# Normalising the second block's windowed attention after the fact: one inversion for all sums, spread by matmul during the merge gates

## The chip, the cores and the metric

The program runs on one core of one Trainium2 chip. The metric is the device time of one execution, in microseconds (us). The engines run side by side, each through its own queue in order: TensorE (PE, with weight loads shown apart as PEld), VectorE (DVE), ScalarE (ACT), GpSimd (POOL) and the queue that issues most transfers (SP). They meet only at semaphores.

## The reference

Two blocks run one after the other on a sequence of 512 tokens of width 1024. The change lies in the second one: a windowed attention with 16 query heads on 4 key heads, whose softmax has a learned sink in its denominator, and the gated merge behind it.

```python
def one_block(args):                      # one block of 128 queries; q, k, v of 64 per head
    s_loc = einsum('bqkrd,bskd->bkrqs', qn, kn) * scale, masked to the window
    s_ctx = einsum('bqkrd,bskd->bkrqs', qn, k_ctx) * scale
    logits = concatenate([s_loc, s_ctx])
    m = maximum(max(logits), sink_l)
    p = exp(logits - m)
    denom = sum(p) + exp(sink_l - m)
    return einsum('bkrqs,bskd->bqkrd', p / denom, vals)
...
y_b = window_gqa(qh, kh, vh, k_ctx, v_ctx, attn_sink)
g_a, g_b = split(sigmoid(h @ w_in[gates] + b_merge_gate))
merged = g_a * (y_a @ w_proj_a) + g_b * (y_b @ w_proj_b)
x = x + g1 * (merged @ w_out)
# then: router, top-64 tokens for each of 16 experts, expert products, final norm
```

`p / denom` may be formed behind the product with the values as well, since `denom` belongs to a query and a head alone.

## The kernel before

**The attention loop.** It walks 16 units: 4 key heads by 4 blocks of 128 queries. A unit has four query heads and a window of `nb` = 4 blocks of keys (first and last query block) or 5. Work of three units overlaps. In step i of the loop each engine does, in this order:

- PE: scores of unit i, first pair of heads (`att_scores`, L1167 and L1178); two turns (transposes, L1201) of the probabilities of unit i-1; scores of the second pair; the other turns; then `att_values` of unit i-2 (L1221). At its end, before: four fp32 matmuls (L1228), which spread the reciprocals of the four heads' sums over 64 partitions and 128 queries, into the other half of the bank that holds the values. In the trace each fp32 matmul leaves two records.
- DVE: the inversion of unit i-1's sums (`att_recip`, L2551 and L2552), mask and maximum of unit i (L2534, L2535, L2539), the sink's argument (L2543), some evictions of turned probabilities (L2558), then `att_out` of unit i-2: a copy of the values (L2567) and the multiplication by the spread reciprocals (L2568). Units 4 to 7 in addition have a quarter of `gate_low` each (L2575).
- ACT: three evictions of turned probabilities (L1917), four exponentials with their sums (L1907), the sink's exponential (L1913); in four steps a quarter of `gate_high` (L1927).

The last steps of the loop hold the first three tiles of the first merge gate (`first_gate`), so that PE has work while the last probabilities come.

**The merge behind it.** Eight products in the order of `MERGE`: gate a 0, gate a 1, gate b 0, gate b 1, proj a 0, proj a 1, proj b 0, proj b 1. Each is four tiles of 24 matmuls (L810; 8 steps of k by three products of rounded parts). Each product's 128 x 4096 weights are split first: ACT writes the rounded high part (L1552), DVE the rest, the low part (L2039), and PE waits for `low_ready`. There are two slots for high parts that take turns: the split for product n+1 is begun on ACT when product n-1 is done on PE. ACT evicts the gate tiles with a sigmoid (L1484). DVE has nothing between the splits until the branches are rounded at the fourth gate product.

**PSUM banks.** `plan_banks` gives each tile of the merge, in order, the next of eight banks. `claim` makes PE wait until the tile that had the bank before is evicted (`freed_a`, `freed_d` count ACT's and DVE's evictions in their order).

## Time and profile before

| | us |
|---|---|
| median of 3 runs | 2354.07 |
| the 3 runs | 2354.07, 2354.26, 2347.15 |
| the profiled execution | 2349.28 |
| its span on the core | 2346.8 |
| the attention loop in it | 1038 to 1181 |
| the merge and out projection in it | 1181 to 1399 |
| routing and experts in it | 1399 to the end |

What lies outside the profiled span is 2349.28 - 2346.8 = 2.5 us. PE is busy 95% of the span, DVE 40%, ACT 26%, POOL 6%; the mean granted TensorE clock is 0.98 of full speed. Such a share is an average over stages, so the text below reads the attention loop and the gate products by themselves: first how busy each engine is there, then the chain of work that ended last, then single instructions in order of time.

### The profile page before, as it was taken

To read this page: it belongs to the slowest core of one execution; us is meant where nothing else is said; L and a number is where in the kernel's file an instruction comes from. 1 tells how busy PE (TensorE), PEld (TensorE's weight loads), DVE (VectorE), ACT (ScalarE), POOL (GpSimd) and SP (SyncE) were. 2 spreads that over 40 slices of the span, in tenths; PEclk is the share of its full clock that TensorE was granted. 3 is DMA by queue.
4 is the path that set the end of the run, shared out by engine and by line. 5 is a ranking of instruction groups with operands and counts; after the bars stand their busy time and mean duration, and the time that the engine had idled before them with its cause. 6 is when DMAs were issued, how large, how long until landed. Compare 5 with 4: busy or idle time off the path is not lost.

```text
span 2346.8 us, 25253 instructions
## 1 busy us (share of the span) xinstructions
PE 2223.7 (95%) x10940; PEld 1465.5 (62%) x10940; DVE 947.9 (40%) x1313; ACT 603.4 (26%) x858; POOL 143.8 (6%) x138
## 2 busy tenths in 40 slices
PE   7999999999999999999999998999898989898998
PEld 5887888878888888887788883434242424242433
DVE  4848435478887353798624322111111101110011
ACT  5315233343333254336533221000000000000001
POOL 0231000310000010320000210000000000000000
PEclk9999999999999999999999998999999999999999
DMA  7220434435454342220023249999999999999997
GB/s 307 105 78 32 166 144 179 161 144 205 160 209 170 118 144 101 88 72 1 1 72 108 96 193 365 429 435 430 430 433 430 429 433 430 430 432 431 429 430 296
DMA packets 55948, 571.88 MB, mean 244 GB/s; under 512 B 3808, under 2 KB 3936, under 8 KB 36000
## 3 DMA queue, kind: packets, MB, share of 16 engines
q1 hardware_dynamic: 51392, 524.55, 54.1%
q0 software_dynamic: 3152, 28.71, 3.3%
q10 hardware_dynamic: 1296, 17.04, 1.9%
q8 instruction: 86, 1.41, 0.2%
q14 instruction: 22, 0.18, 0.0%
HBM read 568.18 MB, written 2.10 MB: 243 GB/s over the span
## 4 chain that ended last, share of the span: by engine, by line
PE 36%; DMA 18%; DVE 3%; ACT 1%; issue 1%; DVEq 0%; SPq 0%; ACTq 0%
PE ps L1359 10%; PE ps L810 9%; DMA arena<-in_w_exp_up 8%; PE ps L1455 6%; DMA arena<-in_w_exp_gate 4%; DMA weights<-in_w_exp_gate 3%; PE ps L1332 3%; DVE arena L2156 2%; DMA weights<-in_w_exp_down 1%; PE ps L1201 1%; PE ps L1221 1%; DMA weights<-in_w_exp_up 1%; PE ps L1379 1%; PE ps L1167 1%; PE ps L1400 1%
## 5 line engine op out<-in xcount | busy, mean ns | idle before, releaser
L810 PE MATMUL ps<-weights_r 128*128 128x512 f32 (+1 forms) x2656 | 813.5, 386 | 8.2 <-DVE hT_r L2059 4.3
L810 PEld LDWEIGHTS ps<-weights_r 128*128 128x128 f32 x2656 | 495.5, 188 | 114.9 <-issue 7.9
L810 PE MATMUL ps<-hT_r,weights_r 128*128 128x512 f32 x1264 | 462.0, 390 | 0.0
L1359 PE MATMUL ps<-weights,arena 128*64 128x512 f32 x768 | 352.1, 615 | 50.7 <-DMA weights<-in_w_exp_up 36.6
L1361 PE MATMUL ps<-weights,arena 128*64 128x512 f32 x768 | 352.4, 616 | 0.0
L2039 DVE TENSOR_TENSOR weights_r<-weights,weights_r 128x4096 fp32r<-128x4096 f32 (+1 forms) x45 | 192.7, 4282 | 223.0 <-ACT weights_r L1552 221.2
L1359 PEld LDWEIGHTS ps<-weights,arena 128*64 128x64 f32 x768 | 105.6, 141 | 283.1 <-issue 246.5
L810 PEld LDWEIGHTS ps<-hT_r,weights_r 128*128 128x128 f32 x1264 | 237.7, 188 | 48.8
L810 PE MATMUL ps<-arena_r,weights_r 128*128 128x512 f32 (+1 forms) x768 | 243.8, 387 | 0.0
L1552 ACT ACTIVATE weights_r<-weights 128x4096 fp32r<-128x4096 f32 (+1 forms) x46 | 161.6, 3512 | 217.4 <-PE ps L810 114.5
L2711 DVE TENSOR_TENSOR hT<-hT,ps 128x512 f32<-128x512 f32 x32 | 22.0, 688 | 438.9 <-PE ps L1361 438.9
L1455 PE MATMUL ps<-weights,hT 128*64 128x512 f32 x384 | 168.6, 594 | 0.6 <-DMA weights<-in_w_exp_down 0.6
L1458 PE MATMUL ps<-weights,hT 128*64 128x512 f32 x384 | 168.5, 594 | 0.0
L810 PEld LDWEIGHTS ps<-arena_r,weights_r 128*128 128x128 f32 x768 | 144.2, 188 | 29.3
L1359 PE MATMUL ps<-arena 128*64 128x512 f32 x248 | 112.8, 608 | 16.3 <-DMA arena<-in_w_exp_up 13.3
L1455 PEld LDWEIGHTS ps<-weights,hT 128*64 128x64 f32 x384 | 51.1, 137 | 109.1 <-issue 105.9
L1361 PE MATMUL ps<-arena 128*64 128x512 f32 x256 | 116.2, 608 | 0.0
L2696 DVE SCALAR_TENSOR_TENSOR xT<-ps,mod_cols,xT 128x512 f32<-128x512 f32 x56 | 42.0, 751 | 165.8 <-PE ps L1379 160.6
L1361 PEld LDWEIGHTS ps<-weights,arena 128*64 128x64 f32 x768 | 105.7, 141 | 0.0
L2078 DVE SCALAR_TENSOR_TENSOR weights<-weights,arena 128x1024 f32<-128x1024 f32 x80 | 94.3, 1224 | 13.5 <-DMA weights<-in_w_ada 11.0
L1999 ACT ACTIVATE hT<-ps 128x512 f32<-128x512 f32 x32 | 16.5, 599 | 292.6 <-PE ps L1400 292.6
L1359 PEld LDWEIGHTS ps<-arena 128*64 128x64 f32 x248 | 33.8, 140 | 91.5 <-issue 66.3
(326 smaller groups left out, 2379.6 us busy)
## 6 DMA issues: line engine op xcount, KB each, us to landing
weights<-in_w_exp_down SPq DMA_DIRECT2D x21, 4096.0 KB, 31.6
weights<-in_w_exp_gate SPq DMA_DIRECT2D x21, 4096.0 KB, 27.5
weights<-in_w_exp_up SPq DMA_DIRECT2D x21, 4096.0 KB, 28.5
weights<-in_w_in SPq DMA_DIRECT2D x18, 2048.0 KB, 7.9
arena<-in_w_exp_down SPq DMA_DIRECT2D x7, 4096.0 KB, 31.7
arena<-in_w_exp_gate SPq DMA_DIRECT2D x7, 4096.0 KB, 31.1
arena<-in_w_exp_up SPq DMA_DIRECT2D x7, 4096.0 KB, 31.4
weights<-in_w_up SPq DMA_DIRECT2D x11, 2048.0 KB, 8.0
```

Source lines behind the costliest of these rows:

```text
L810: last = pe.matmul(t, a if w_first else b, b if w_first else a, start=(k == 0 and n == 0), stop=(k == kt - 1 and n == len(pairs) - 1))
L1167: local = pe.matmul(ps[:, c:c + w], q2[o:o + 64, 2 * kv + p, n * P:(n + 1) * P], kdup[o:o + 64, kv, b0 * P:b1 * P], start=True, stop=True)
L1332: last = pe.matmul(bank(6, 2)[:, d * P:(d + 1) * P], h2_tok[:, t, 256 * j + r:256 * j + 256:2], sels[it % 2][:, t, :], start=(t == 0), sto ...
L1359: la = pe.matmul(bank(b0 + n)[0:64, :], xe[:, 2 * j + r, 0:64], ra[:, n * 512:(n + 1) * 512], start=start, stop=stop)
L1361: lb = pe.matmul(bank(b0 + n)[64:128, :], xe[:, 2 * j + r, 64:128], rb[:, n * 512:(n + 1) * 512], start=start, stop=stop)
L1455: la = pe.matmul(bank(4 + hh)[0:64, :], hmid_t[:, 4 * j + r, 0:64], w[:, r, 0, hh * 512:(hh + 1) * 512], start=(j + r == 0), stop=(j == ST ...
L1458: lb = pe.matmul(bank(4 + hh)[64:128, :], hmid_t[:, 4 * j + r, 64:128], w[:, r, 1, hh * 512:(hh + 1) * 512], start=(j + r == 0), stop=(j = ...
L1552: A(slots_r[high_slot(i)][:, 0:n], slots[sl][:, 0:n], ACT.Copy).then_inc(S["high_ready"], 1)
L2039: ve.tensor_tensor(slots_r[sl][:, 0:n], slots[sl][:, 0:n], slots_r[high_slot(i)][:, 0:n].bitcast(F32), ALU.subtract).then_inc(S["low_ready ...
L2078: last = ve.scalar_tensor_tensor(w[:, j, :], w[:, j, :], 1.0, rows[:, 0, :], ALU.mult, ALU.mult, accum_out=cc[:, 4 * c + j, 0:1])
L2156: last = ve.tensor_tensor(rsinbuf[q:q + 32, i % 2, :], plain[o:o + 32, :], cs[o:o + 32, 1, :], ALU.mult)
L2696: ve.scalar_tensor_tensor(xT[:, d, :], ps[:, b * 512:(b + 1) * 512], mod_cols2[:, 40 + d, 0:1], xT[:, d, :], ALU.mult, ALU.add).then_inc(S ...
```

## The change

The new code keeps the values of every unit as they come from PSUM (`att_out` is one copy) and keeps all maxima and sums of the 16 units in the arena (`neg_m`, `den`, 4 blocks by 16 heads each). Behind the loop `att_recips` on DVE and `att_sinks` on ACT form all 64 denominators per query at once, invert them, and split the result in a high and a low part. `turn_reciprocals` on PE turns both (32 rows: 16 high, 16 low) into one bank, ACT evicts it as `rden_t`, and behind the second gate product `spread_reciprocals` multiplies it with a matrix of ones and zeros (`head_sel`), one fp32r matmul for each of the eight 128-row tiles of the values. `scale_values` on DVE multiplies these tiles, straight from PSUM, into the values. ACT's rounding of the branch waits for that.

```diff
@@ plan_banks, merge
             for n in range(4):
                 b.add((tag, kind, part, nq, n), "A" if kind == "gate" else "D")
+            if (tag, i) == ("m2", 0):
+                b.add("rdenT", "A")
+                b.skip(7)
+            if (tag, i) == ("m2", 1):
+                for k in range(KT):
+                    b.add(("rden", k), "D")
@@ PE, merge
                         feature_tiles(name, tiles[done:], h_parts, c0=done * P)
+                        if (tag, i) == ("m2", 0):
+                            turn_reciprocals()
+                        if (tag, i) == ("m2", 1):
+                            spread_reciprocals()
@@ PE, att_values
-                pe.wait_ge(S["r_ready"], i + 1)
-                for a in range(2):
-                    for g in range(2):
-                        r = 2 * a + g
-                        last = pe.matmul(t[64 * g:64 * g + 64, 256 + a * P:256 + (a + 1) * P],
-                                         rden[:, i % 2, r:r + 1].broadcast_to([P, 64]), ident,
-                                         start=True, stop=True)
+            def turn_reciprocals():
+                pe.wait_ge(S["r_ready"], 1)
+                t = claim(pe, "rdenT")
+                for n in range(TT):
+                    last = pe.transpose(t[0:2 * NH, n * P:(n + 1) * P], unit_rows[:, n, :], ident)
+                fill("rdenT", last)
+            def spread_reciprocals():
+                wait_freed(pe, "rdenT")
+                for k in range(KT):
+                    sel = head_sel[0:2 * NH, 2 * k:2 * k + 2, :].rearrange("p h d -> p (h d)")
+                    fill(("rden", k), pe.matmul(claim(pe, ("rden", k)), sel, rden_t[0:2 * NH, :],
+                                                start=True, stop=True))
@@ ACT, merge_gates
+                    if (tag, i) == ("m2", 0):
+                        free("rdenT", "A", A(rden_t[0:2 * NH, :], wait_full(act_e, "rdenT")[0:2 * NH, :], ACT.Copy))
...
-                            act_e.wait_ge(S["pv_free"], UNITS)
+                            wait_freed(act_e, ("rden", KT - 1))
@@ ACT, attention
-                    if i >= 2:
-                        act_e.wait_ge(S["r_ready"], i - 1)
...
-            def att_sink(i):
-                act_e.wait_ge(S["sink_arg"], i + 1)
-                act_e.wait_ge(S["exp_done"], 4 * i + 4)
-                A(sink_e[:, i % 2, :], sink_t[:, i % 2, :], ACT.Exp).then_inc(S["sink_exp"], 1)
+            def att_sinks():
+                act_e.wait_ge(S["sink_arg"], 1)
+                A(neg_m, neg_m, ACT.Exp).then_inc(S["sink_exp"], 1)
+                act_e.wait_ge(S["den_summed"], 1)
+                A(rden_high, den, ACT.Copy).then_inc(S["rden_high"], 1)
...
+            att_sinks()
             act_e.wait_ge(S["pv_full"], 2 * UNITS)
             merge_gates("m2", 3)
@@ DVE, merged_tiles
                     prepare((tag, kind, part, nq))
+                    if (tag, i) == ("m2", 2):
+                        scale_values()
@@ DVE, attention
-            def att_recip(i):
-                ve.wait_ge(S["sink_exp"], i + 1)
...
-                link(ve.tensor_tensor(rden[:, i % 2, :], den[:, i % 2, :], sink_e[:, i % 2, :], ALU.add))
-                ve.reciprocal(rden[:, i % 2, :], rden[:, i % 2, :]).then_inc(S["r_ready"], 1)
+            def att_recips():
+                ve.wait_ge(S["nm_ready"], 2 * UNITS)
+                ve.wait_ge(S["exp_done"], 4 * UNITS)
+                ve.tensor_tensor(neg_m, neg_m, wide(sink.unsqueeze(1), P, TT, NH), ALU.add)   # sink_arg
+                ve.tensor_tensor(head_sel[0:2 * NH, :, :], ...)                               # 32 x 1024
+                ve.wait_ge(S["sink_exp"], 1)
+                link(ve.tensor_tensor(den, den, neg_m, ALU.add))
+                ve.reciprocal(den, den).then_inc(S["den_summed"], 1)
+                ve.wait_ge(S["rden_high"], 1)
+                ve.tensor_tensor(rden_low, den, rden_high.bitcast(F32), ALU.subtract).then_inc(S["r_ready"], 1)
+            def scale_values():
+                ve.wait_ge(S["pv_free"], UNITS)
+                for k in range(KT):
+                    t = wait_full(ve, ("rden", k))
+                    free(("rden", k), "D", ve.tensor_tensor(q2[:, k, :], t, q2[:, k, :], ALU.mult))
@@ DVE, att_out
-                link(ve.tensor_copy(v, t[:, 0, :, :]))
-                ve.tensor_tensor(v, v, t[:, 1, :, :], ALU.mult).then_inc(S["pv_free"], 1)
+                ve.tensor_copy(q2[:, 2 * kv:2 * kv + 2, n * P:(n + 1) * P],
+                               ps[:, 7 * 512:7 * 512 + 256].rearrange("p (a q) -> p a q", a=2)).then_inc(
+                    S["pv_free"], 1)
```

PE's queue at the end of the loop and around the first gate products, before (L1221 values of the last unit, L1228 their reciprocals, L810 gate tiles; the rows with waits are the heads of tiles 2 and 3 of gate a 0, tile 0 of gate a 1, and tile 0 of gate b 0):

```order
L1221 MATMUL ps<-weights,arena 64x256 [waits pv_free,at_kept_d,at_kept_a]
L1221 MATMUL ps<-weights,arena 64x256 x7
L1228 MATMUL ps<-cst,small 64x128 [waits r_ready]
L1228 MATMUL ps<-cst,small 64x128 x3
L810 MATMUL ps<-weights_r 128x512 [waits freed_a,low_ready]
...
L810 MATMUL ps<-weights_r 128x512 [waits freed_d,low_ready]
...
L810 MATMUL ps<-weights_r 128x512 [waits freed_a,low_ready]
```

The same queue of the changed kernel (L1234 values, L819 gate tiles, L1245 the turn, L1253 the spreading), first to the head of gate a 1, then to the head of gate b 0:

```order
L1234 MATMUL ps<-weights,arena 64x256 [waits pv_free,at_kept_d,at_kept_a]
L1234 MATMUL ps<-weights,arena 64x256 x7
L819 MATMUL ps<-weights_r 128x512 [waits freed_a,low_ready]
...
L1245 MATMUL ps<-cst,arena 32x128 [waits freed_d,r_ready]
L1245 MATMUL ps<-cst,arena 32x128 x3
L819 MATMUL ps<-weights_r 128x512 [waits freed_a,low_ready]
...
L1253 MATMUL ps<-arena_r 128x512 [waits freed_a] x8
L819 MATMUL ps<-weights_r 128x512 [waits freed_d,low_ready]
```

The four matmuls of each unit are gone, four transposes and eight spreading matmuls stand between the gate products, and gate b 0 now waits for a bank that DVE frees. In the plan that bank is the one of `("rden", 0)`; gate a 1 takes the bank of `rdenT`, which ACT frees.

DVE's queue from the last values on, before (L2567 and L2568 values, L2039 low parts of the weights, L2181 the first branch):

```order
L2567 COPY arena<-ps 128x2x128 [waits pv_full]
L2568 TENSOR_TENSOR arena<-arena,ps 128x2x128 [waits dve_chain]
L2039 TENSOR_TENSOR weights_r<-weights,weights_r 128x4096 [waits high_ready] x4
L2181 TENSOR_TENSOR arena_r<-arena,arena_r 128x512 [waits branch_high] x4
L2181 TENSOR_TENSOR arena_r<-arena,weights_r 128x512 [waits branch_high] x4
```

and of the changed kernel (L2570 to L2578 are `att_recips`, L2063 the low parts, L2585 is `scale_values`):

```order
L2598 COPY arena<-ps 128x2x128 [waits pv_full] x2
L2570 TENSOR_TENSOR arena<-arena,small 128x4x16 [waits exp_done,nm_ready]
L2572 TENSOR_TENSOR arena_r<-cst 32x1024
L2575 TENSOR_TENSOR arena<-arena 128x4x16 [waits sink_exp]
L2576 RECIPROCAL arena<-arena 128x4x16 [waits dve_chain]
L2578 TENSOR_TENSOR arena_r<-arena,arena_r 128x4x16 [waits rden_high]
L2063 TENSOR_TENSOR weights_r<-weights,weights_r 128x4096 [waits high_ready] x3
L2585 TENSOR_TENSOR arena<-ps,arena 128x512 [waits tile_full,pv_free]
L2585 TENSOR_TENSOR arena<-ps,arena 128x512 [waits tile_full] x7
L2063 TENSOR_TENSOR weights_r<-weights,weights_r 128x4096 [waits high_ready]
```

The eight multiplications stand behind three low parts: those for gate a 1, gate b 0 and gate b 1. On ACT the two new instructions (L1935, L1937) stand between the last eviction of probabilities and the high part for gate a 1.

## Rows read from the trace of the kernel before

**Rows 1.** Page: granted TensorE clock, tenths of full speed, 40 slices of 58.7 us.
```profile
PEclk9999999999999999999999998999999999999999
```
**Rows 2.** Windows: us, busy time (x records) of each engine, granted clock, DMA share, GB/s.
```profile
1060.00:1100.00 40.00, 38.03 (x318) 28.37 (x320) 32.89 (x67) 29.32 (x69) 0.00 (x0) 1.00 0.00 1
1195.00:1215.00 20.00, 20.00 (x90) 16.57 (x89) 4.43 (x1) 4.52 (x6) 0.00 (x0) 1.00 0.23 87
```
**Rows 3.** Chain that ended last, one unit: start us, us, what.
```profile
1137.52 0.44 PE ps L1228 x8
...
1142.41 0.61 ACT arena L1917
1143.01 0.14 issue
1143.15 1.95 PE ps L1221 x16
1145.10 0.44 PE ps L1228 x8
```
**Rows 4.** Timeline, seam between two units: start us, us, engine, line, operation.
```profile
1096.64 2.38 PE L1221 MATMUL ps<-weights,arena 128*64 128x256 f32 x20
1098.82 0.64 PE L1228 MATMUL ps<-cst,small 128*64 128x128 f32 x8
1099.39 0.70 PE L1167 MATMUL ps<-arena 64*128 64x256 f32 x4
```
**Rows 5.** Timeline, end of the attention loop and first gate product.
```profile
1181.27 3.63 ACT L1552 ACTIVATE weights_r<-weights 128x4096 fp32r<-128x4096 f32 x1 [11.05 <-PE ps L1228]
1181.27 0.42 DVE L2567 COPY arena<-ps 128x256 f32<-128x256 f32 x1 [7.17 <-PE ps L1228]
1184.94 4.42 DVE L2039 TENSOR_TENSOR weights_r<-weights,weights_r 128x4096 fp32r<-128x4096 f32 x1 [2.78 <-ACT weights_r L1552]
1192.38 0.69 ACT L1484 ACTIVATE arena<-ps,cols 128x512 f32<-128x512 f32 x1 [4.32 <-PE ps L810]
```
**Rows 6.** Timeline, seam between gate a 1 and gate b 0.
```profile
1208.70 0.69 ACT L1484 ACTIVATE arena<-ps,cols 128x512 f32<-128x512 f32 x1 [4.75 <-PE ps L810]
1214.14 0.69 ACT L1484 ACTIVATE arena<-ps,cols 128x512 f32<-128x512 f32 x1 [4.75 <-PE ps L810]
1214.73 3.62 ACT L1552 ACTIVATE weights_r<-weights 128x4096 fp32r<-128x4096 f32 x1
1218.38 4.43 DVE L2039 TENSOR_TENSOR weights_r<-weights,weights_r 128x4096 fp32r<-128x4096 f32 x1 [17.33 <-ACT weights_r L1552]
```
**Rows 7.** Single lines: duration ns min/median/max, first and last start us, forms.
```profile
L2204 DVE TENSOR_TENSOR arena<-ps,arena x32: 684/692/692, 387.9 to 1344.8; 128x512 f32<-128x512 f32 x32
L1960 ACT ACTIVATE hT<-ps x1: 587/587/587, 1404.6 to 1404.6; 16x512 f32<-16x512 f32 x1
L2325 DVE RECIPROCAL arena<-arena x8: 3342/3344/3347, 181.8 to 224.0; 128x512 f32<-128x512 f32 x8
L2575 DVE TENSOR_TENSOR weights_r<-weights,weights_r x4: 1218/1218/1219, 1092.6 to 1115.6; 128x1024 fp32r<-128x1024 f32 x4
```
**Rows 8.** Windows (columns as in rows 2): PE idle, then at work again.
```profile
1036.00:1038.00 2.00, 1.05 (x9) 0.88 (x9) 1.75 (x5) 1.92 (x6) 0.00 (x0) 1.00 0.00 0
1052.00:1053.00 1.00, 1.00 (x6) 1.00 (x6) 0.00 (x0) 1.00 (x4) 0.00 (x0) 0.50 0.00 0
1406.00:1407.00 1.00, 1.00 (x10) 1.00 (x9) 0.93 (x4) 1.00 (x3) 0.00 (x0) 0.87 0.88 377
1686.00:1687.00 1.00, 1.00 (x6) 0.29 (x4) 0.00 (x0) 0.00 (x0) 0.00 (x0) 0.92 0.84 360
```
**Rows 9.** Timeline, first matmuls behind three waits of PE; in brackets idle us and releaser.
```profile
1050.15 0.92 PE L1167 MATMUL ps<-arena 64*128 64x384 f32 x4 [1.80 <-ACT weights L1907]
1402.06 1.02 PE L1284 MATMUL ps<-cst,arena 128*16 128x128 f32 x4 [1.27 <-DVE arena L2624]
1682.42 0.84 PE L1359 MATMUL ps<-weights,arena 128*64 128x512 f32 x1 [2.54 <-DMA weights<-in_w_exp_up]
```

More of the change, by code:

```diff
@@ L333, in build_two_blocks @@
             merged_ready pair_in0 pair_in1 pair_in2 pair_in3 up_halves_in conv_mid gelu_ready act_ready ln_ready ln_stats ln_root ya_ready exp_done
-            kdup_ready as_half as_full nm_ready sink_arg sink_exp at_full at_kept_a at_kept_d
+            kdup_ready as_half as_full nm_ready sink_arg sink_exp at_full at_kept_a at_kept_d den_summed rden_high
             r_ready pv_full pv_free row_ready aff_exp router_in router_w aff_ready rank_ready sel_ready wsel_full
@@ L699, in build_two_blocks @@
         nsink = small[:, 64:80]
-        neg_m, den, sink_e, rden, sink_t = (small[:, 80 + 8 * j:88 + 8 * j].rearrange("p (b r) -> p b r", b=2)
-                                            for j in range(5))
+        unit_rows, unit_rows_r = at(17920, TT, 2 * NH), at(17920, TT, 2 * NH, rounded=True)
+        den, neg_m = unit_rows[:, :, 0:NH], unit_rows[:, :, NH:2 * NH]
+        rden_low, rden_high = unit_rows_r[:, :, 0:NH], unit_rows_r[:, :, NH:2 * NH]
+        head_sel = at(16896, NH, HD, rounded=True)
+        rden_t = at(16384, L, rounded=True)
         tops = small[:, 120:124].rearrange("p (b g) -> p b g", b=2)
@@ L1220, in att_values @@
                     for g in range(2):
-                        pe.matmul(t[64 * g:64 * g + 64, 0:256].rearrange("p (a q) -> p a q", a=2),
-                                  vals[:, kv * HD:(kv + 1) * HD], pt[:, g, b, :, :],
-                                  start=(b == 0), stop=(b == nb - 1))
-                pe.wait_ge(S["r_ready"], i + 1)
-                for a in range(2):
-                    for g in range(2):
-                        r = 2 * a + g
-                        last = pe.matmul(t[64 * g:64 * g + 64, 256 + a * P:256 + (a + 1) * P],
-                                         rden[:, i % 2, r:r + 1].broadcast_to([P, 64]), ident,
-                                         start=True, stop=True)
-                        if a == 1:
-                            last.then_inc(S["pv_full"], 1)
+                        last = pe.matmul(t[64 * g:64 * g + 64, 0:256].rearrange("p (a q) -> p a q", a=2),
+                                         vals[:, kv * HD:(kv + 1) * HD], pt[:, g, b, :, :],
+                                         start=(b == 0), stop=(b == nb - 1))
+                        if b == nb - 1:
+                            last.then_inc(S["pv_full"], 1)
+            def turn_reciprocals():
[10 more added lines that the diff above has]
+                                                start=True, stop=True))
             def first_gate(n):
@@ L2536, in att_max @@
                                       ps[:, c:c + 2 * nb * P].rearrange("p (g s) -> p g s", g=2), AX.X, ALU.max))
-                if i >= 2:
-                    ve.wait_ge(S["sink_exp"], i - 1)
-                ve.scalar_tensor_tensor(neg_m[:, i % 2, 2 * p:2 * p + 2], tops[:, p, :], -1.0, nsink[:, h:h + 2],
+                ve.scalar_tensor_tensor(neg_m[:, n, h:h + 2], tops[:, p, :], -1.0, nsink[:, h:h + 2],
                                         ALU.mult, ALU.min).then_inc(S["nm_ready"], 1)
-                if p:
-                    ve.wait_ge(S["nm_ready"], 2 * i + 2)
-                    ve.tensor_tensor(sink_t[:, i % 2, :], neg_m[:, i % 2, :], sink[:, 4 * kv:4 * kv + 4],
-                                     ALU.add).then_inc(S["sink_arg"], 1)
-            def att_recip(i):
-                ve.wait_ge(S["sink_exp"], i + 1)
-                if i >= 2:
-                    ve.wait_ge(S["pv_full"], 2 * (i - 1))
-                link(ve.tensor_tensor(rden[:, i % 2, :], den[:, i % 2, :], sink_e[:, i % 2, :], ALU.add))
-                ve.reciprocal(rden[:, i % 2, :], rden[:, i % 2, :]).then_inc(S["r_ready"], 1)
+            def att_recips():
+                ve.wait_ge(S["nm_ready"], 2 * UNITS)
+                ve.wait_ge(S["exp_done"], 4 * UNITS)
+                ve.tensor_tensor(neg_m, neg_m, wide(sink.unsqueeze(1), P, TT, NH), ALU.add).then_inc(
+                    S["sink_arg"], 1)
+                ve.tensor_tensor(head_sel[0:2 * NH, :, :], wide(ident[0:2 * NH, 0:NH].unsqueeze(2), 2 * NH, NH, HD),
+                                 wide(ident[0:2 * NH, NH:2 * NH].unsqueeze(2), 2 * NH, NH, HD), ALU.add)
+                ve.wait_ge(S["sink_exp"], 1)
[8 more added lines that the diff above has]
+                    free(("rden", k), "D", ve.tensor_tensor(q2[:, k, :], t, q2[:, k, :], ALU.mult))
             def att_keep(i, u):
@@ L2592, in _ @@
                     late_context_keys()
-                if 0 < i <= UNITS:
-                    att_recip(i - 1)
                 if i < UNITS:
@@ L2606, in _ @@
                     gate_low(i - 6)
+            att_recips()
             merged_tiles("m2")
```

6 lines of the change are left out of this document (2 added, 4 removed).

## The prediction

> **What bounds the kernel now.** I read the stage of the change first, by windows. In the attention loop PE is busy 38.03 of 40 us, DVE 32.89, ACT 29.32, and the granted clock is full; between the gate products behind it PE is busy all the time [rows 2]. So PE sets the pace in both, and what it is spared or made to do counts. The remaining 5% of the loop is in the chain that ended last [rows 3]: in each unit it runs on PE, leaves it for one eviction on ACT (0.61 us and 0.14 of issue), and comes back for the values and the four matmuls of L1228 (eight records). These stand in the chain with 0.44 us in 14 of the 16 units (the rows show two of them). The two others are the first, where DVE's and ACT's work is the chain, and the one at 1161, behind which PE waited for the last exponentials in any case. Outside this stretch I need the page's clock line (full nearly throughout [rows 1]) only to know that a dip there would be new. The experts' stage streams weights, but PE's progress frees its buffers and the routing in front of it is serial, so I let a shift of PE at 1181 or 1214 go through to the end undiminished.
>
> **What goes from the loop.** Four matmuls per unit. The timeline gives more than the chain's 0.44: their first record starts at 1098.82, the next scores at 1099.39, that is 0.57 us of PE's queue [rows 4]. The values' records in front run at (1098.82 - 1096.64) / 20 = 0.109 us each, with no gap before L1228, while 0.14 us of the 0.57 lie between the last of L1228 and the scores. The switch to the scores may need that gap behind the values too; but their weights could also be loaded while the values still run, since their waits are over by then. I take 0.57, with 0.44 and 0.66 (the same seam counted from the weight loads) as ends. 14 units: 14 x 0.57 = **8.0 us gained** (6.2 to 9.2).
>
> The Trainium skill speaks for less: its page "TensorE: Matmul & The Clock Gate", section "Wait — 56ns, not 53.3ns?", has back-to-back matmuls of 128 columns start 55.6 ns apart at full clock. Eight would take 0.44 us, as the chain says and not as the starts say; by it the gain would be 6.2 us.
>
> DVE is spared a 128 x 256 multiplication and three small instructions a unit, ACT one exponential. Neither is the bound, so I count nothing; where ACT stands in the chain (four units with a quarter of a high part) up to 1.5 us more may come, kept for the range. DVE also gets slack, so it does not become late next when PE goes 0.57 us faster per unit of 8: it has 7 us in 40 to spare already [rows 2].
>
> **What comes between the loop and gate a 1.** In the changed order ACT's high part for gate a 1 stands behind two instructions that hang on DVE, and DVE's denominators behind the last copy of values. Before, both started at 1181.27 and the low part was ready at 1184.94 + 4.42 = 1189.4, while PE needed it at about 1192.0 (0.4 us before ACT evicts tile 3, 1192.38 [rows 5]): 2.6 us to spare. Now ACT starts after: the copy 0.42, a small sum 0.2, `head_sel` (32 x 1024; nearest row 1.22 [rows 7]), another small sum 0.2, a reciprocal of 64 columns (3.344 / 512 x 64 = 0.42, with a fixed part some 0.55 [rows 7]), a small copy 0.25, and six handoffs of 0.05: 3.1 us later. That alone would use up the slack and 0.5 us more. But PE itself comes later: four transposes, then gate a 1 takes the bank of `rdenT`, which ACT evicts behind tile 3. So 1192.38 + 0.69 + 0.587 (a 16 x 512 eviction [rows 7]) + 0.05 = 1193.7 against 1192.0, on the old clock of times. The wait for the bank covers the late low part: **1.7 us lost**, about 1.2 of it idle. Lower end 1.2, if the eviction of 32 rows overlaps the sigmoid's end; if `head_sel` took 0.5 more, the cover would still hold.
>
> **What comes between gate a 1 and gate b 0.** Eight spreading matmuls of 512 columns: 20 us hold 90 of that width [rows 2], so 8 x 0.222 = 1.8 us of work. They fill all eight banks. Gate b 0 then needs the bank of `("rden", 0)`, and DVE frees it behind its third low part, that of gate b 1. That low part can't be early: its high part goes into the slot that gate a 1 has just left, so ACT begins it at 1214.73, behind its last gate tile, and DVE ends it at 1218.38 + 4.43 = 1222.81 [rows 6]. One multiplication from PSUM is 0.692 [rows 7], with 0.05 to hand over 1223.55. Before, PE went on at about 1214.14 - 0.4 = 1213.74. So **9.8 us lost**, 8.0 of them idle. The next tiles aren't held: DVE frees a bank every 0.69 us, and a tile takes 1214.14 - 1208.70 = 5.44. The ends are near, 9.4 and 10.1, since every row is one that runs in this place today. Later splits keep their slack: in this row the low part is ready 13 us before gate b 1.
>
> **The clock behind the stall.** After the idle 1.80 us that end at 1050.15, PE's clock was at half at 1052; after the wait that ended at 1682.42 it was back at full shortly into the window from 1686, 3.7 us later, and after the one that ended at 1402.06 shortly into the window from 1406, some 4.2 us later [rows 8, 9]. Eight idle us will do the same: some 3.8 us at 1.2 instead of 2.4 GHz, in which half the work is done, **1.9 us lost** (1.6 to 2.1). In front of gate a 1 the idle 1.2 us lie between a gap of 0.95 us with the clock at full (1036 to 1038) and the one of 1.80 that was followed by half [rows 8, 9]; I take none and keep 1.6 for the range.
>
> **Sum.** -8.0 + 1.7 + 9.8 + 1.9 = **+5.4 us**. On the profiled execution, whose span leaves 2.5 us outside as I expect it to stay, 2349.28 + 5.4 = 2354.7; the median of the runs lies 4.8 higher, and the forecast for a median is 2354.07 + 5.4 = **2359.5 us**, 0.23% slower. That lies within 0.3% (7.1 us), about what a measurement of this kernel can tell from no change. The ends: 9.2 + 1.5 gained against 1.2 + 9.4 + 1.6 gives +1.5; 6.2 gained against 1.7 + 1.6 + 10.1 + 2.1 gives +9.3.
>
> **Rivals.**
> - *The pace of the seam.* If the switch from values to scores keeps its gap of 0.14 us, the gain is 14 x 0.44 = 6.2 and the sum +7.2: 2361.3, just beyond the line. The chain's 0.44 and the skill's rule speak for it; that the scores' weights load beside the running values speaks against. 0.12.
> - *A second clock dip (slower).* PE's clock falls at the bank wait in front of gate a 1 as well, and the first half of tile 0 runs at 1.2 GHz: 1.6 more, +7.0 to +7.2, 2361.2. It decides when that idle gap is nearer to 1.8 than to 0.95 us, or when the late low part makes it longer. 0.14.
> - *No stall.* DVE has the banks free in time, since ACT's high part or the order on DVE is earlier than I read them. Then -8.0 + 1.7 + 1.8 = -4.5: 2349.6. The rows on DVE's queue speak against it. 0.07.
> - *Absorbed.* The weight stream sets the end whatever PE does at 1214: about 2354. Its start on freed buffers speaks against. 0.05.
> - *More comes free in the loop*, 5 us and over, with little stall: below 2347. 0.03.
>
> My forecast has 0.59. Some of it (0.04) lies beyond 0.3% by its own ends. So slower 0.12 + 0.14 + 0.04 = 0.30, faster 0.04 (with a little for a low base), within 0.3% 0.66.
>
> **The range.** The sum's ends on the level of the runs: the four executions have a mean of 2351.2, so +1.5 would be about 2352, and an absorbed stall may show 2351; above, 2354.3 + 9.3 = 2363.6. I give 2351 to 2364, which leaves out the cases without the stall and the corners where both slower rivals meet.
>
> **What would show it.** The loop from first scores to the last values 8 us shorter, with scores starting 0 to 0.14 us behind the values; ACT's high part for gate a 1 about 3.1 us behind the last values; a gap of PE of about 1.2 us in front of gate a 1, named as ACT's eviction; one of about 8 us in front of gate b 0, named as DVE's `scale_values`, with the clock at half behind it; everything from gate b 0 on as before. I would be wrong at the root if the first `scale_values` ran before the low part of gate b 1, or if the loop's units kept their length.

## The result, and the profile after

The changed kernel takes 2358.29 us in the median of 7 runs (2357.73 to 2360.7). The kernel before, run beside it, takes 2352.62 us (7 runs, 2347.15 to 2354.26). The ratio is 1.0028, with a 95% interval of 1.0018 to 1.0038: about 5.7 us slower, just inside the 0.3% of the prediction. The forecast was 2359.5 us, +5.4.

The profiled execution of after took 2360.58 us (span 2358.5), that of before 2349.28 (span 2346.8). These two differ by 11.3 us (their spans by 11.7), twice what the medians do, so I compare stages first. "Loop" is from the first scores of the second attention to the start of gate a 0's third tile (the first gate product behind the last values). "Gates" is from there to ACT's eviction of the last gate tile. Each kernel was profiled a second time. All in us:

| trace | loop | gates | half clock at the loop's start |
|---|---|---|---|
| before | 143.13 | 76.53 | yes |
| before, second execution | 143.07 | 76.54 | yes |
| after | 136.27 | 89.53 | yes |
| after, second execution | 135.26 | 90.30 | no |

The first executions of both have the half clock at the loop's start, so they are compared: the loop is 6.9 us shorter, the gates 13.0 us longer, together +6.1. That is near what the medians show. The rest of the 11.7 us lies outside: 0.5 in front of the loop (where the clock was at half for as long in both), and 3.2 in the products behind the gates and 2 at the start of the experts, both in stretches where the granted clock was half for longer. The second execution of before has the 3.2 too (below), and as much half clock at the experts' start as after (23.9 us, for 20.5 in the first of before); it took 2359.38 us. They belong to the execution, not to the change.

The gates of after's second execution are 0.8 us longer than those of the first. All of it lies behind the wait in front of gate b 0, where the clock stayed at half for longer (the experiment with 128 rows).

The page of after, busy us of each engine and the clock line (before: [rows 1]), shows little of all this:
```profile
PE 2228.3 (94%) x10824; PEld 1462.3 (62%) x10824; DVE 941.8 (40%) x1262; ACT 600.2 (25%) x845; POOL 143.5 (6%) x138
...
PEclk9999999999999999999999998999999999999999
```
The windows do. Columns: stretch, its us, busy us (and records) of PE, PE's weight loads, DVE, ACT and POOL, granted clock, DMA share, GB/s. The first two stand beside those of [rows 2]:
```profile
1060.00:1100.00 40.00, 37.92 (x296) 26.81 (x293) 31.37 (x49) 29.28 (x65) 0.00 (x0) 1.00 0.01 2
1195.00:1215.00 20.00, 16.34 (x72) 12.88 (x70) 1.53 (x2) 5.57 (x4) 0.00 (x0) 0.93 0.21 76
1213.00:1214.00 1.00, 0.00 (x0) 0.00 (x0) 0.44 (x1) 0.53 (x1) 0.00 (x0) 0.50 1.04 403
1219.00:1220.00 1.00, 1.00 (x3) 0.81 (x3) 1.00 (x3) 0.00 (x0) 0.00 (x0) 0.50 0.00 0
1223.00:1224.00 1.00, 1.00 (x6) 0.80 (x6) 0.00 (x0) 0.00 (x0) 0.00 (x0) 1.00 0.00 0
```
In the loop PE holds fewer records in about the same busy time: 296 for 318. It moves faster through the units and is still the fullest engine. Between the gates its 20 us are no longer full: it idles from 1211.3, the clock falls to half, stays there when work starts again (three records in the us from 1219, six in that from 1223), and is full by 1223.

The timeline names the places. Columns: start us, us, engine, line, operation, out and in, form; in brackets the idle time before and who ended it. The seam between values and scores (before: [rows 4]):
```profile
1094.71 2.38 PE L1234 MATMUL ps<-weights,arena 128*64 128x256 f32 x20
1097.02 0.70 PE L1180 MATMUL ps<-arena 64*128 64x256 f32 x4
```
The way into gate a 1 (before: [rows 5]):
```profile
1174.75 0.50 PE L819 MATMUL ps<-weights_r 128*128 128x512 f32 x1
...
1175.36 1.21 DVE L2572 TENSOR_TENSOR arena_r<-cst 32x1024 fp32r<-32x1024 f32 x1
1176.74 0.55 DVE L2576 RECIPROCAL arena<-arena 128x64 f32<-128x64 f32 x1
1177.49 3.61 ACT L1574 ACTIVATE weights_r<-weights 128x4096 fp32r<-128x4096 f32 x1
1181.13 4.43 DVE L2063 TENSOR_TENSOR weights_r<-weights,weights_r 128x4096 fp32r<-128x4096 f32 x1 [3.29 <-ACT weights_r L1574]
1185.76 0.60 PE L1245 MATMUL ps<-cst,arena 128*32 128x128 f32 x4
1186.54 0.57 ACT L1642 ACTIVATE arena_r<-ps 32x512 fp32r<-32x512 f32 x1
1187.26 0.47 PE L819 MATMUL ps<-weights_r 128*128 128x512 f32 x1 [0.90 <-ACT arena_r L1642]
```
And the one into gate b 0 (before: [rows 6]):
```profile
1209.23 2.11 PE L1253 MATMUL ps<-arena_r 32*128 32x512 f32 x8
1209.92 3.60 ACT L1574 ACTIVATE weights_r<-weights 128x4096 fp32r<-128x4096 f32 x1
1213.56 4.43 DVE L2063 TENSOR_TENSOR weights_r<-weights,weights_r 128x4096 fp32r<-128x4096 f32 x1 [18.47 <-ACT weights_r L1574]
1217.90 4.87 DVE L2585 TENSOR_TENSOR arena<-ps,arena 128x512 f32<-128x512 f32 x8
1218.73 0.77 PE L819 MATMUL ps<-weights_r 128*128 128x512 f32 x1 [7.39 <-DVE arena L2585]
```
PE has spread the inverses by 1211.3. DVE, which must read each spread bank before it can be reused, had been idle for 18.47 us, but its next instruction in order is the low part of gate b 1 (L2063), which waits for ACT's high part (L1574) of the same weights. The multiplications stand behind it. So PE waits 7.39 us for two instructions that gate b 0 doesn't need.

### The profile page after: what moved, and what is told of

It reads as the page before. It is cut to its first block, busy times and chain, and to the rows that moved or that the text cites. A ratio compares the mean times of both kernels' runs of the same rounds, so it can differ in the third digit from the quotient of the medians.

```text
span 2358.5 us, 24875 instructions
## 1 busy us (share of the span) xinstructions
PE 2228.3 (94%) x10824; PEld 1462.3 (62%) x10824; DVE 941.8 (40%) x1262; ACT 600.2 (25%) x845; POOL 143.5 (6%) x138
## 4 chain that ended last, share of the span: by engine, by line
PE 35%; DMA 17%; DVE 4%; ACT 1%; issue 1%; DVEq 0%; SPq 0%; ACTq 0%
PE ps L1381 11%; PE ps L819 9%; DMA arena<-in_w_exp_up 8%; PE ps L1477 5%; DMA weights<-in_w_exp_gate 4%; PE ps L1354 3%; DMA arena<-in_w_exp_gate 3%; DVE arena L2180 2%; PE ps L1401 1%; DMA weights<-in_w_exp_down 1%; DMA weights<-in_w_exp_up 1%; PE ps L1214 1%; PE ps L1234 1%; PE ps L1180 1%; PE ps L1422 1%
## 5 line engine op out<-in xcount | busy, mean ns | idle before, releaser
L819 PE MATMUL ps<-weights_r 128*128 128x512 f32 (+1 forms) x2656 | 817.4, 387 | 17.2 <-DVE arena L2585 7.4
L819 PEld LDWEIGHTS ps<-weights_r 128*128 128x128 f32 x2656 | 497.8, 189 | 126.0 <-DVE weights_r L2063 12.2
L819 PE MATMUL ps<-hT_r,weights_r 128*128 128x512 f32 x1264 | 462.7, 390 | 0.0
L1381 PE MATMUL ps<-weights,arena 128*64 128x512 f32 x768 | 357.5, 623 | 50.6 <-DMA weights<-in_w_exp_up 36.0
L1383 PE MATMUL ps<-weights,arena 128*64 128x512 f32 x768 | 357.7, 623 | 0.0
L2063 DVE TENSOR_TENSOR weights_r<-weights,weights_r 128x4096 fp32r<-128x4096 f32 (+1 forms) x45 | 193.0, 4289 | 229.9 <-ACT weights_r L1574 228.1
L819 PEld LDWEIGHTS ps<-hT_r,weights_r 128*128 128x128 f32 x1264 | 238.3, 189 | 48.7
L819 PE MATMUL ps<-arena_r,weights_r 128*128 128x512 f32 (+1 forms) x768 | 244.9, 388 | 0.0
L1574 ACT ACTIVATE weights_r<-weights 128x4096 fp32r<-128x4096 f32 (+1 forms) x46 | 161.5, 3511 | 208.5 <-PE ps L819 114.3
L819 PEld LDWEIGHTS ps<-arena_r,weights_r 128*128 128x128 f32 x768 | 144.8, 189 | 29.7 <-issue 0.2
L2102 DVE SCALAR_TENSOR_TENSOR weights<-weights,arena 128x1024 f32<-128x1024 f32 x80 | 94.2, 1222 | 13.0 <-DMA weights<-in_w_ada 10.5
```

The lines of the kernel that those rows point to most:

```text
L819: last = pe.matmul(t, a if w_first else b, b if w_first else a, start=(k == 0 and n == 0), stop=(k == kt - 1 and n == len(pairs) - 1))
L1381: la = pe.matmul(bank(b0 + n)[0:64, :], xe[:, 2 * j + r, 0:64], ra[:, n * 512:(n + 1) * 512], start=start, stop=stop)
L1383: lb = pe.matmul(bank(b0 + n)[64:128, :], xe[:, 2 * j + r, 64:128], rb[:, n * 512:(n + 1) * 512], start=start, stop=stop)
L1574: A(slots_r[high_slot(i)][:, 0:n], slots[sl][:, 0:n], ACT.Copy).then_inc(S["high_ready"], 1)
L2063: ve.tensor_tensor(slots_r[sl][:, 0:n], slots[sl][:, 0:n], slots_r[high_slot(i)][:, 0:n].bitcast(F32), ALU.subtract).then_inc(S["low_ready ...
L2102: last = ve.scalar_tensor_tensor(w[:, j, :], w[:, j, :], 1.0, rows[:, 0, :], ALU.mult, ALU.mult, accum_out=cc[:, 4 * c + j, 0:1])
```

## The experiments

**1 to 5: undo one piece of the change.** Theory: the loss is the order on DVE (the low part ahead of the multiplications), the idle time and the half clock behind it; the loop itself gains. Rivals: the loop gains little; the wait is only a symptom of some slower stage.

*DVE multiplies first.* The call stands ahead of the split's preparation:
```diff
+                    if (tag, i) == ("m2", 2):
+                        scale_values()
                     ...prepare of the split...
-                    if (tag, i) == ("m2", 2):
-                        scale_values()
```


> The changed kernel with one move: DVE runs scale_values before the low part of gate b 1 instead of behind it. Theory (order on DVE): the banks of the spread reciprocals come free while PE still spreads, the 7.4 us wait in front of gate b 0 goes and with it the half clock behind it; 9.7 - 1.9 + 1.7 = 9.5 us under the changed kernel, about 3.8 us under the kernel before (ratio 0.998). Rival 1 (the stall belongs to the high part or the transfer of the weights, not to the place on DVE): as the changed kernel, 5.7 us over before. Rival 2 (the clock behind the stall costs nothing by itself): 2.1 us under before.

Measured: 2348.29 us (12 runs), 0.9976 of the kernel before (0.9964 to 0.9989), so 10.0 us below after, and 4.9 below the median of 29 runs of before (2353.23). Loop 135.27 (without the half clock at its start), gates 80.35: 9.2 below after's gates, and 3.8 above those of before, for the turned and spread inverses. The stages so give 3 us under before, or 4 where the half clock at the loop's start is missing; the medians' 4.9 is more than they account for, within its interval (2.6 to 8.5). The timeline at gate b 0:
```profile
1208.14 2.11 PE L1253 MATMUL ps<-arena_r 32*128 32x512 f32 x8
...
1208.74 4.88 DVE L2585 TENSOR_TENSOR arena<-ps,arena 128x512 f32<-128x512 f32 x8 [14.71 <-PE ps L1253]
1208.84 3.62 ACT L1574 ACTIVATE weights_r<-weights 128x4096 fp32r<-128x4096 f32 x1
1210.19 0.50 PE L819 MATMUL ps<-weights_r 128*128 128x512 f32 x1
...
1213.53 4.42 DVE L2063 TENSOR_TENSOR weights_r<-weights,weights_r 128x4096 fp32r<-128x4096 f32 x1
```
The multiplications run while ACT makes the high part, PE goes from the spread to the gate product without a gap, and the low part ends at 1217.95, that is 44.3 us behind the start of gate a 0's third tile, 1.0 us later than in after (43.2). Gate b 1 needs it only four tiles after 1210.19, so this costs nothing. The wait cost everything and bought nothing. This version is faster than both kernels.

*The loop's part alone.* Values stay undivided; no turned, spread or multiplied inverses:
```diff
-            if (tag, i) == ("m2", 0):
-                b.add("rdenT", "A")
...
-                            spread_reciprocals()
...
-                        scale_values()
...
-            att_recips()
```


> Only the loop's part of the change: the four matmuls, the inversion and the multiplication per unit are gone and nothing takes their place, so the values stay undivided and the output is not the reference's. Theory: about 6.9 us under the kernel before, all of it in the loop (0.49 us for each of 14 units), ratio 0.997. Rival (chain figure, 0.44 a unit): 6.2 us. Rival (a shift of PE at this place is absorbed by the weight stream later): no difference from before, and the changed kernel's whole loss would then be something else.

Measured: 2346.31 us, 0.9968 (0.9957 to 0.9979). Loop 135.25 (without the half clock at its start), gates 76.49, which is before's 76.53 to 0.04. The loop's gain is real and lies in the loop alone.

*The turn one tile earlier,* with the multiplications first as above. The four transposes come in front of gate a 0's last tile, so that ACT evicts `rdenT` before it is wanted:
```diff
+                if (tag, i, n) == ("m2", 0, 3):
+                    b.skip(1)
+                    b.add("rdenT", "A")
+                    b.skip(6)
...
+                            if (tag, i, n) == ("m2", 0, 3):
+                                free("rdenT", "A", A(rden_t[0:2 * NH, :], ...))
```


> As e1_scale_first, and the transposes of the reciprocals stand in front of the first gate product's tile 3, into a bank that gate a 1 needs one tile later; ACT evicts it before tile 3's gate. Theory: the 0.9 us that PE waited for ACT's eviction go, 1.1 to 1.2 us in all, leaving 0.5 us for the transposes: 4.9 us under the kernel before. Rival (the late low part of gate a 1 takes the bank wait's place): 0.5 us or less better than e1_scale_first, and PE waits for L2063 there.

Measured: 2349.71 us, 0.9978 (0.9967 to 0.9990). In the trace the step works: the first eviction of gate a 1 comes 17.12 us after the start of gate a 0's third tile, for 18.24 in the version above and 16.69 in before, and the gates take 79.22 for 80.35. The medians (2348.29 and 2349.71) don't show this 1.1 us; the intervals overlap.

*PE kept busy through the wait, by 32 rows.* 33 more of the last spreading matmul; what they write is the same value again:
```diff
+                    for _ in range(33 if k == KT - 1 else 0):
+                        pe.matmul(claim(pe, ("rden", k)), sel, rden_t[0:2 * NH, :], start=True, stop=True)
```


> The changed kernel with its order and its wait for the bank, but PE repeats the last spreading matmul 33 times (7.4 us, the same result into the same bank) instead of standing idle. Theory (the clock's own cost): gate b 0 starts when it did, but at full clock, and 1.6 to 2.0 us go: 3.9 us over before. Rival (the half clock is not caused by the idle time, or costs nothing): as the changed kernel, 5.7 us over before.

Measured: 2364.01 us, 1.0048 (1.0033 to 1.0063), above every expectation. I had meant to keep the clock up. It fell all the same, as its timeline and windows show:
```profile
1210.19 11.32 PE L1254 MATMUL ps<-arena_r 32*128 32x512 f32 x33
1221.86 0.80 PE L819 MATMUL ps<-weights_r 128*128 128x512 f32 x1
```
```profile
1210.00:1212.00 2.00, 2.00 (x10) 1.60 (x9) 0.00 (x0) 2.00 (x1) 0.00 (x0) 1.00 0.93 314
1212.00:1214.00 2.00, 2.00 (x9) 1.61 (x8) 1.20 (x1) 0.76 (x1) 0.00 (x0) 0.89 1.04 402
1214.00:1216.00 2.00, 2.00 (x6) 1.56 (x5) 2.00 (x1) 0.00 (x0) 0.00 (x0) 0.50 0.81 306
```
PE is busy all of each 2 us, yet the clock is at half from 1214. At half clock the filler lasts longer than the wait it should fill, and delays gate b 0 itself: it starts 47.85 us behind gate a 0's third tile, for 43.98 in after. The run doesn't price the clock, but it shows something that I didn't know (last section).

*The same by 128 rows,* reading `h_high` in place of the 32 rows:
```diff
-                        pe.matmul(claim(pe, ("rden", k)), sel, rden_t[0:2 * NH, :], start=True, stop=True)
+                        pe.matmul(claim(pe, ("rden", k)), h_high[:, 0, 0:P], h_high[:, 0, :], start=True, stop=True)
```


> As e4_warm_pe, but the 33 matmuls that fill PE's wait use all 128 rows of the array (a product of the rounded h with itself, overwritten by the last spreading matmul) instead of 32. In e4's trace the clock fell while PE was busy with the 32-row matmuls. Theory (what the clock follows is how much of the array works, not whether PE has an instruction): the clock stays at 2.4 GHz, gate b 0 starts 44.0 us behind the start of gate a 0's tile 2, as in the changed kernel, and the last gate tile is evicted 1.6 us earlier: 4.1 us over the kernel before. Rival (the clock falls for any repeated matmul there): as e4_warm_pe, some 11 us over before.

Measured: 2358.72 us, 1.0021 (1.0011 to 1.0030). Here the clock stays full:
```profile
1212.00:1214.00 2.00, 2.00 (x10) 1.65 (x10) 2.00 (x1) 0.00 (x0) 0.00 (x0) 1.00 1.05 397
...
1216.00:1218.00 2.00, 2.00 (x9) 1.23 (x8) 2.00 (x5) 0.00 (x0) 0.00 (x0) 1.00 0.00 0
```
```profile
1216.86 0.50 PE L819 MATMUL ps<-weights_r 128*128 128x512 f32 x1
...
1222.64 0.69 ACT L1508 ACTIVATE arena<-ps,cols 128x512 f32<-128x512 f32 x1 [11.42 <-PE ps L819]
```
In after, first and second execution, the same place:
```profile
1226.20 0.69 ACT L1506 ACTIVATE arena<-ps,cols 128x512 f32<-128x512 f32 x1 [12.68 <-PE ps L819]
```
```profile
1220.44 0.77 PE L819 MATMUL ps<-weights_r 128*128 128x512 f32 x1 [7.39 <-DVE arena L2585]
1228.68 0.69 ACT L1506 ACTIVATE arena<-ps,cols 128x512 f32<-128x512 f32 x1 [13.44 <-PE ps L819]
```
From the start of gate b 0 to its first eviction are 5.78 us here (1222.64 - 1216.86), 7.47 in the first execution of after (1226.20 - 1218.73) and 8.24 in the second (1228.68 - 1220.44). The half clock behind the wait costs 1.69 us in one execution and 2.46 in the other. The wait itself remains, and with it the time. Gate b 0 even starts 0.45 us later here (44.43 us behind gate a 0's third tile, for 43.98), since one spreading matmul stands behind the filler. So the gates are 1.2 us shorter than in after's first execution (88.29 for 89.53), and the medians of after and of this version (2358.29 and 2358.72) are too near to show that.

**6 to 10: what in the loop brings the gain?** Theory after the first runs: only PE's four matmuls a unit. Rival: DVE or ACT holds part of it back.

*Only the matmuls dropped.* The kernel before without L1228, its wait for the reciprocals, and the count moved to the last values matmul:
```diff
-                pe.wait_ge(S["r_ready"], i + 1)
-                for a in range(2):
-                    for g in range(2):
-                        r = 2 * a + g
-                        last = pe.matmul(t[64 * g:64 * g + 64, 256 + a * P:256 + (a + 1) * P],
-                                         rden[:, i % 2, r:r + 1].broadcast_to([P, 64]), ident,
-                                         start=True, stop=True)
```


> The kernel before without the four matmuls per unit and PE's wait for the reciprocals; DVE and ACT keep everything they did (DVE multiplies by what happens to lie in the bank, so the output is not the reference's). Theory (PE alone sets the loop's pace): the same gain as e2_loop_only has, 6.9 us with the clock dip at the loop's start and 7.8 without, since DVE's and ACT's relief counts for nothing. Rival (part of the gain is the work taken from DVE and ACT): clearly less than e2_loop_only, about 5 us.

Measured: 2349.75 us, 0.9987 (0.9975 to 0.9999). Loop 138.92, without the half clock at its start; the loop of after without it is 135.26. So PE alone doesn't set the pace. The theory fell. In the loop's window (columns as above) PE is down to 36.64 us of 40 and DVE up to 34.18, and the timeline shows a turn of PE (L1201) that starts behind DVE's multiplication, since that hands back the bank it writes to:
```profile
1060.00:1100.00 40.00, 36.64 (x279) 25.67 (x280) 34.18 (x69) 29.50 (x68) 0.00 (x0) 1.00 0.01 2
```
```profile
1093.64 0.70 PE L1167 MATMUL ps<-arena 64*128 64x256 f32 x4
1095.10 0.42 DVE L2561 TENSOR_TENSOR arena<-arena,ps 128x256 f32<-128x256 f32 x1
1095.67 0.63 PE L1201 MATMUL ps<-cst,arena 128*128 128x128 f32 x4 [0.15 <-ACT arena L1900]
```
The trace names ACT as the releaser, but by the code the bank's last user is L2561, which ended at 1095.52, just where the idle 0.15 us begin. PE's wait for this bank (L1197) has records of its own. This one starts at 1095.56, 0.04 us behind the end of L2561. In after such records stand as close behind the copy, but it ends early enough: in seven places of the loop the turn starts 0.38 to 0.43 us behind the start of the matmul before it here, and 0.11 to 0.21 in after. PE's waits in the loop (us in total, times, longest) have a line of DVE's that after and before don't have; L2551 is in this kernel DVE's eviction of turned probabilities (L2558 in before):
```profile
PE ps L1221 <- DVE weights L2551: 0.8, 3, 0.3
```
The lengths of single steps show it without any releaser. A step is counted from the first values matmul of one unit to that of the next, in us:

| step | before | matmuls dropped | after |
|---|---|---|---|
| unit 4 to 5 | 7.71 | 7.71 | 7.03 |
| unit 5 to 6 | 7.38 | 6.94 | 6.89 |

Of the 15 steps, seven get 0.4 to 0.5 us shorter by the dropped matmuls alone, which is 3.1 of the 3.2 us that this version gains. The other eight keep their length. Seven of these (to units 1, 4, 5, 8, 9, 12 and 13) are 0.3 to 0.7 us shorter in after, where DVE and ACT do less as well, and one, in which PE waits for the last exponentials, is as long in all three.

*A second execution of each kernel,* without an edit.

> A second trace of the kernel before. Between the last gate tile's eviction and the end of the last norm (n4) the first trace took 141.3 us, the changed kernel 144.5 and e1 to e4 142.9 to 143.0, with a stretch of half clock at its end. If that is chance of the execution (theory), this trace may show 141.3 or 143; if it belonged to the change, it would show 141.3 again.

> A second trace of the changed kernel. Theory: the loop and the gate products take what they took, 136.2 and 89.5 us (or 0.9 less in the loop if the dip at its start is missing), and the 3.2 us behind them and 2 us at the experts' start are smaller or elsewhere. Rival (they belong to the change): 144.5 us again from the last gate tile to n4.

Measured: before 2359.38 us (span 2356.9), after 2359.64 (span 2357.5). The stages stand in the table above. Two stretches vary from execution to execution: the half clock at the loop's start (absent in the second of after; 136.27 - 135.26 = 1.01 us), and one behind the gates, in the first of after and then in the second of before. The first price holds in the other traces with after's loop: 136.20 and 136.28 with the half clock (fillers by 32 and by 128 rows), 135.25 to 135.31 in the four without. The second stretch, in after and in before:
```profile
1380.00:1392.00 12.00, 12.00 (x57) 10.36 (x56) 0.75 (x1) 0.63 (x1) 1.26 (x1) 0.72 0.36 154
```
```profile
1378.00:1392.00 14.00, 14.00 (x69) 12.25 (x68) 1.50 (x2) 1.00 (x2) 1.26 (x1) 0.76 0.34 144
```
PE is busy throughout in both. From the last gate tile to the next norm's sums the first of before took 141.34 us, the second 144.53, the first of after 144.50, the second 142.9, and after with the filler by 64 rows (next) 141.3. Nothing of this 3.2 us is the change's.

*The filler by 64 rows* (`h_high[0:64, ...]`), run once.

> As e4 and e5, with 33 matmuls that use 64 of the array's rows. The clock fell with 32 rows and stayed with 128. If it follows the share of the array that works, 64 rows with 128 columns may go either way: at half clock the 33 matmuls take 11 us or more and gate b 0 begins 47 to 48 us behind the start of tile 2 (e4: 47.9), at full clock 44.4 (e5).

Measured: 2357.61 us. The clock stays full, gates 88.27 (88.29 by 128 rows, 94.2 by 32):
```profile
1218.00:1220.00 2.00, 2.00 (x10) 1.66 (x9) 2.00 (x1) 0.00 (x0) 0.00 (x0) 1.00 0.84 315
```

*The multiplication alone dropped,* the matmuls kept:
```diff
-                link(ve.tensor_copy(v, t[:, 0, :, :]))
-                ve.tensor_tensor(v, v, t[:, 1, :, :], ALU.mult).then_inc(S["pv_free"], 1)
+                ve.tensor_copy(v, t[:, 0, :, :]).then_inc(S["pv_free"], 1)
```


> The kernel before without DVE's multiplication L2568 alone (the values stay undivided, the output is not the reference's); the four matmuls, the inversion and the sink stay. Measured by the loop, from the first scores to the start of gate a 0's tile 2: 143.1 us in both traces of before. Theory (with the matmuls in PE's queue PE is the bound, and DVE's work is cover): 142 to 143 us. Rival (the bank's return by DVE already limits PE): 140 or less.

*Both dropped* (this edit and that of the matmuls).

> e6_drop_matmuls_only (138.9 us in the loop) and in addition without DVE's multiplication L2568; inversion and sink stay. Theory (the second of DVE's two steps holds the bank that the next turn needs, and the following maxima): the loop comes near e2_loop_only's 135.2 us, 136 or less. Rival (what holds PE up is the inversion with its waits for the sink's exponential): 138 or more.

*Matmuls and the per-unit inversion dropped,* the multiplication kept:
```diff
-                    if i >= 2:
-                        act_e.wait_ge(S["r_ready"], i - 1)
...
-                if 0 < i <= UNITS:
-                    att_recip(i - 1)
```


> e6_drop_matmuls_only (138.9 us in the loop) without the inversion (L2551, L2552) and ACT's wait for it; the multiplication and the sink's exponential stay (the output is not the reference's). The other half of the question of e9_drop_both: if the inversion and its wait for ACT hold PE up, 136 or less; if the multiplication does, 138 or more.

Measured, with the loop's length on one footing (where the half clock stood at its start, 1.01 is taken off, the difference of after's two executions; in before that is worked out, not measured):

| version | loop | on one footing | one run, us |
|---|---|---|---|
| before | 143.13 | 142.12 | |
| multiplication dropped | 142.60 | 141.59 | 2352.08 |
| matmuls dropped | 138.92 | 138.92 | |
| matmuls and inversion dropped | 137.82 | 137.82 | 2349.55 |
| matmuls and multiplication dropped | 137.57 | 137.57 | 2345.99 |
| the loop's part alone | 135.25 | 135.25 | |

With PE's matmuls in place, DVE's multiplication is worth 0.5 us. Once they are gone it is worth 1.35, and the inversion 1.1. So the theory for the multiplication alone held (142 to 143 us), and of the two that expected 136 or less or else 138 or more, neither did: both loops lie between. From the matmuls alone (3.2) to the whole (6.9) are 3.7 us that come from DVE and ACT. PE's waits for L2551, which stands behind the inversion in DVE's order, fit: 0.8 us with the matmuls dropped, 0.7 with the multiplication dropped too, none without the inversion. Multiplication and inversion would make up 2.45 of the 3.7 if they add; the 1.2 left I can't lay on single instructions. The remaining edits (the sinks' sum, ACT's exponential) were not tried apart.

## Why the prediction was right, and where its steps weren't

The total came out at +5.7 for +5.4, and the forecast of a time 0.23% longer, within 0.3%, held. Part by part:

- **The loop, -8.0.** Measured -6.9 for like executions. The step that failed is the seam's price, 0.57 us a unit. From the first values matmul to the next scores were 2.75 us before and are 2.31 now: 0.44 saved, and the gap of 0.13 us now stands behind the values (20 x 0.109 = 2.18). That is the price of the rival "pace of the seam", 14 x 0.44 = 6.2. The Trainium skill's 55.6 ns between matmuls of 128 columns ("TensorE: Matmul & The Clock Gate", section "Wait — 56ns, not 53.3ns?") spoke for it too, and the trace agrees, with 0.44 us for eight records. I argued that the scores' weights could load under running values; the gap stayed. That 6.2 comes near 6.9 is in part luck: step by step the gain isn't 0.44 fourteen times, but 0.4 to 0.5 in seven steps and 0.3 to 0.7 in seven that needed DVE and ACT as well.
- **"Neither is the bound, so I count nothing"** for DVE and ACT. Wrong as a statement, though the sum hardly shows it. Dropping PE's matmuls alone gives 3.2 us, not 6.2 or 8.0: without the relief of DVE the next bank and the next weights come late. The 7 us in 40 that I called slack are an average, and half of the steps have places where PE waits for DVE, with the rest of that slack elsewhere. DVE's multiplication was worth little while PE's matmuls stood in the queue (0.5), and the work taken from DVE and ACT was needed for more than half of the gain (3.7 of 6.9) once they were gone.
- **In front of gate a 1, +1.7.** Measured +1.6 (18.27 for 16.69 us from gate a 0's third tile to the first eviction), with PE idle for 0.90 instead of 1.2 us, released by ACT as named. The low part was ready at 1181.13 + 4.43 = 1185.56, when PE needed it at 1187.26: covered, as said. ACT's high part began 2.60 us behind the last copy's start (1177.49 - 1174.89), for 3.1 forecast. `head_sel` took 1.21 for 1.22, the reciprocal 0.55 for 0.55. No clock dip here, so the rival of the second dip is out, for a gap of 0.90 us:
```profile
1187.00:1188.00 1.00, 0.74 (x3) 0.67 (x4) 0.00 (x0) 1.00 (x2) 0.00 (x0) 1.00 0.71 111
```
- **Between gate a 1 and gate b 0, +9.8, of it 8.0 idle.** Measured 9.50 from the first spreading matmul (1209.23) to gate b 0 (1218.73), 7.39 of it idle, by the releaser that was named. Against before, gate b 0 starts 11.2 us later behind gate a 0's third tile (43.98 for 32.81), of which 1.6 are gate a 1's: 9.6 for this place. PE starts when the first of DVE's multiplications is done, 0.83 us behind the start at 1217.90.
- **The clock behind the wait, +1.9.** The version by 128 rows gives 1.69 for the profiled execution. There the clock was back at full by 1223, some 4 us behind the start, where the rows of two other places had said 3.7 and 4.2. In the second execution the clock was at half for over 5 us behind the same wait (0.50 in the us from 1224, 1.00 in that from 1226, for a start at 1220.44), and the price was 2.46, outside the 1.6 to 2.1 that I had allowed. So this term isn't one number, and that the first execution met it is in part luck.
- **The gates as a whole** had 1.7 + 9.8 + 1.9 = 13.4 forecast and 13.0 measured, the loop -8.0 and -6.9. So the sum of what was measured is +6.1. In the second execution of after the gates are 13.8 longer than before's, and the sum, with the half clock at the loop's start on one footing, is +7.0. The forecast's 5.4 is nearer to the medians' 5.7 than its parts deserve.
- **"Absorbed", "no stall"** are out: the loss in the gates went through to the medians undiminished, and moving DVE's instructions gave it back: 7.39 us idle and 1.69 of clock make 9.1, the gates got 9.2 shorter, and the medians fell by 10.0.

## What to carry to other kernels

When an operation on a side engine frees what the bounding engine needs, look at what stands ahead of it in that engine's order, and whether that can run yet: here one call, moved up past an instruction that was waiting anyway, turned 0.28% lost into 0.24% gained. An engine with 18% of its time free isn't therefore without a say; ask for each unit which of its instructions hands back the bank or buffer that comes next, and cost a removal on the bounding engine with and without that one. Price a removed group of matmuls by its records' own time, and leave the gap at the switch to the next group in place until a trace shows that it goes.

## What the runs showed of the hardware

PE's clock fell to half under matmuls that followed one another without a gap, when each took 32 rows by 128 columns of weights and 512 columns: full at 1210 to 1212, 0.50 from 1214, the filler's 33 in 11.32 us. With 64 or 128 rows in the same place it stayed at 1.00, and 33 by 128 rows took 7.78 us. So "PE is busy" in a profile doesn't say that its clock is safe; the granted clock of the stretch does. The fillers differ in one thing besides the rows: that by 32 rows multiplies by `head_sel`, which holds only ones and zeros, the others by rounded values of h. Rows and contents were not tried apart, so it isn't shown which of the two the clock follows. The eight spreading matmuls of this change are of the 32-row kind. They last 2.1 us, and with the multiplications first they pass at full clock.

Executions of one kernel differ by more than this change is worth: 29 runs of before lie between 2346.0 and 2359.95 us, its two profiled ones at 2349.28 and 2359.38. The gates of these two agree to 0.01 us. What varies is where and for how long the clock is at half (80.3 us in total in the first execution of before, 98.7 in the second, 105.2 in the first of after, 97.6 in the second), with PE busy in some of those stretches. What sets this off was not found.
